# The last feed-forward layer computed in two halves of the tokens, the second half laid between the expert rows

## The reference

```
first_block, twice: x = x + gate * rmsnorm(mixer(h), ...)         # short convolution, then a state-space mixer
                    h = rmsnorm(x, norm_g[i, 2]) * (1 + scale) + shift
                    y = swiglu_ffn(h, f_w_in[i], f_w_out[i])      # width 2816: silu(gate) * up, then back to 1024
                    x = x + gate * rmsnorm(y, norm_g[i, 3])
second_block:       x = x + gate1 * (concat(band attention, gated delta rule) @ w_out)
                    h2 = modulate(rms_norm(x, norm2_gain), shift2, scale2)
                    x = x + gate2 * peer(h2, ...)
```

```
u = expert_down[experts];  vv = expert_up[experts]
act = gelu(einsum("thkd,td->thk", u, hb))
out = einsum("thk,thkd->td", gates * act, vv)
```

## Time and profile before

| | |
|---|---|
| median of 3 runs | 3354.09 us (3353.31 to 3354.44) |
| the profiled execution: span | 3351.2 us, 2.9 us less than the median of the timed runs |
| TensorE busy | 2945.8 us, 88% |
| VectorE busy | 2119.7 us, 63% |
| ScalarE busy | 1400.0 us, 42% |
| GpSimd busy | 652.5 us, 19% |
| read from memory | 793.46 MB, of it 536.90 MB by the gathers |

### The profile page before, as it was taken

How to read it: one execution, slowest core, us unless ns; L and a number is a source line. 1 busy time by engine, 2 the same in 40 slices (tenths; PEclk the granted TensorE clock), 3 DMA queues, 4 the chain that set the end, 5 groups by cost and what they waited for, 6 DMA issues and landing times.

```text
span 3351.2 us, 34609 instructions
## 1 busy us (share of the span) xinstructions
PE 2945.8 (88%) x11990; PEld 2050.0 (61%) x11990; DVE 2119.7 (63%) x3960; ACT 1400.0 (42%) x2879; POOL 652.5 (19%) x575
## 2 busy tenths in 40 slices
PE   6989999899998899998988998878879777777777
PEld 5868888688776688887777753656547232223222
DVE  7655443587786444432552999879669889655555
ACT  3243222444665422224733367772443433333333
POOL 0000000000111000000000133334443444443442
PEclk8999999999998999998998999989989899999999
DMA  6544444244122244442202597989999999999998
GB/s 251 184 144 135 142 141 145 85 151 132 58 70 95 95 139 148 144 129 98 98 26 87 220 371 267 355 341 387 412 420 417 353 421 422 421 422 421 421 421 335
DMA packets 147548, 797.82 MB, mean 238 GB/s; under 512 B 16304, under 2 KB 18480, under 8 KB 81712
## 3 DMA queue, kind: packets, MB, share of 16 engines
q0 software_dynamic: 73728, 536.90, 39.5%
q1 hardware_dynamic: 69840, 251.69, 22.6%
q10 hardware_dynamic: 3808, 7.02, 0.6%
HBM read 793.46 MB, written 2.10 MB: 237 GB/s over the span
## 4 chain that ended last, share of the span: by engine, by line
PE 52%; DMA 20%; DVE 18%; ACT 6%; issue 4%; POOL 0%; DVEq 0%; SPq 0%; POOLq 0%; ACTq 0%
PE psum L153 51%; DMA tail<-in_experts,tail 19%; DVE tail L187 5%; DVE tail L170 2%; ACT L164 2%; DVE tail L182 2%; ACT arena L164 2%; DVE tail L193 1%; DVE arena L182 1%; DVE tail L190 1%; DVE region L170 1%; DVE rounded L170 1%; ACT tail L164 1%; DVE tail L205 1%; DVE tail L196 1%
## 5 line engine op out<-in xcount | busy, mean ns | idle before, releaser
L153 PE MATMUL psum<-tail,arena 128*128 128x256 f32 (+2 forms) x3584 | 1274.5, 505 | 256.2 <-ACT arena L164 235.5
L153 PE MATMUL psum<-rounded,rounded 128*128 128x512 f32 x5496 | 1278.6, 393 | 39.6 <-DVE rounded L182 22.6
L153 PEld LDWEIGHTS psum<-rounded,rounded 128*128 128x128 f32 x5496 | 1034.0, 189 | 262.5 <-issue 29.0
L153 PEld LDWEIGHTS psum<-tail,arena 128*128 128x128 f32 x3584 | 677.7, 199 | 806.1 <-issue 748.4
L187 DVE CUSTOM_DVE_ANT_0 tail<-tail 128x1024 f32<-128x1024 f32 x512 | 621.0, 1223 | 311.7 <-DMA tail<-in_experts,tail 310.4
L216 POOL DMA_INDIRECT tail<-in_experts,tail x512 | 583.6, 1140 | 1015.9 <-PE psum L153 747.0
L164 ACT ACTIVATE tail<-tail 128x1 f32<-128x1 f32 (+1 forms) x1057 | 266.8, 252 | 769.2 <-DVE tail L187 740.7
L170 DVE TENSOR_TENSOR rounded<-arena,rounded 128x1024 fp32r<-128x1024 f32 (+2 forms) x285 | 316.5, 1111 | 333.7 <-ACT rounded L164 333.5
L164 ACT ACTIVATE rounded<-arena 128x1024 fp32r<-128x1024 f32 (+2 forms) x317 | 292.1, 939 | 406.5 <-DVE arena L170 232.5
L164 ACT ACTIVATE arena<-psum 128x256 f32<-128x256 f32 (+2 forms) x210 | 97.5, 480 | 393.6 <-PE psum L153 392.9
L170 POOL TENSOR_TENSOR arena<-arena 128x512 f32<-128x512 f32 x32 | 47.1, 1473 | 1087.7 <-ACT arena L164 1087.7
(11 more groups left out here) (87 smaller groups left out, 1560.4 us busy)
## 6 DMA issues: line engine op xcount, KB each, us to landing
arena<-in_ada SPq DMA_DIRECT2D x136, 512.0 KB, 3.7
arena<-in_fin SPq DMA_DIRECT2D x88, 512.0 KB, 4.2
arena<-in_win SPq DMA_DIRECT2D x56, 512.0 KB, 3.3
arena<-in_fout SPq DMA_DIRECT2D x32, 512.0 KB, 4.1
arena<-in_mxbc SPq DMA_DIRECT2D x32, 512.0 KB, 3.7
arena<-in_pq SPq DMA_DIRECT2D x32, 512.0 KB, 7.8
arena<-in_ain SPq DMA_DIRECT2D x24, 512.0 KB, 4.7
arena<-in_mz SPq DMA_DIRECT2D x16, 512.0 KB, 3.8
```

The source lines that it names most:

```text
L153: return self.e.matmul(o, a, b, start=start, stop=stop, skip_group_check=skip)
```

## The change

- The layer's pieces come twice in the list, once for each half of 256 tokens, in another order: for each pair of tiles two gate pieces, two up pieces, and two pieces of the way back of the pair before. `fout2` holds the way back by its input tile, so that one piece feeds all 8 output tiles, whose sums stay in PSUM banks 4 to 7 through the whole half.
- `pe_half`, `act_half`, `dve_half` do the norm, the 66 pieces and the norm behind, in steps. Half 0 stands where the layer stood. Half 1 is put ahead of main 1, between the rows.
- In half 1, from the fourth piece on, GpSimd writes the low weight parts: `pool_low`, one behind each gather from row 3 to row 65. Loads that reuse a buffer wait for it.
- `steps_of` runs a step behind every row, not every second one, and ranking steps of chunk 1 behind every second row. `EARLY` goes from 6 to 8.
- Main 1 gets the ordinary norm in place of one prepared ahead. Chunk 0's and 1's scores move to ring buffers 5 and 6, so the ring has 6 buffers until row 80 and 7 until row 190. `own_add` gives VectorE other rows. The table of levels is loaded again for main 1.

The diff, cut to its core:

```diff
+        HALF = []
+        for j in range(KF // 2):
+            HALF += [("gate", 2 * j), ("gate", 2 * j + 1), ("up", 2 * j), ("up", 2 * j + 1)]
+            if j:
+                HALF += [("out", 2 * j - 2), ("out", 2 * j - 1)]
+        HALF += [("out", KF - 2), ("out", KF - 1)]
+        SPLIT = list(range(len(PIECES)))
         for f in range(2):
+            if f:
+                AGAIN = len(SPLIT)
+            for what, kk in HALF:
+                SPLIT.append(len(PIECES))
+                piece(("half", f, what, kk), t["fout2"][kk] if what == "out" else t["fin"][1, 2 * kk + (what == "up")])
             for n in range(12):
...
@@ -369,16 +382,31 @@
         former = lambda i: i - 8 if i < 20 else i - 4

         w_in = landed("w_landed", 8)
-        w_hi, w_lo, gemm = signal("w_hi"), signal("w_lo"), signal("gemm")
+        w_hi, w_lo, w_lo_pool, gemm = signal("w_hi"), signal("w_lo"), signal("w_lo_pool"), signal("gemm")
         ada_step, ada_mm, mod_ok = signal("ada_step"), signal("ada_mm"), signal("mod_ok")
         col_in, const_in, x_in = landed("col_landed"), landed("const_landed"), landed("x_landed")
         csil_ok = signal("csil")
         nxt = {}

         def w_tile(p):
-            i = 2048 * (p % 3)
+            q = SPLIT_NO[p]
+            i = 2048 * (q % 3)
             n = 128 * PIECES[p][1]
-            return i, n
+            wf, wr = (w_f, w_r) if q < AGAIN else (w1_f, w1_r)
+            return wf[:, i:i + n], wr[:, i:i + n], wr[:, i + 1024:i + 1024 + n]
+
+        def by_pool(p):
+            return SPLIT_NO[p] >= AGAIN + 3
+
+        def low_at(p):
+            return w_lo_pool.at(p) if by_pool(p) else w_lo.at(p)
+
+        def pool_low(e, p):
+            n = 128 * PIECES[p][1]
+            high, _, low = w_tile(p)
+            e.wait_ge(*w_in.at(("w", p)))
+            e.wait_ge(*w_hi.at(p))
+            e.tt(low, raw[slot_of(NUMBER["w", p])][:, 0:n], high, ALU.subtract).then_inc(*w_lo_pool.tick(p))

         def sp_load(e, i):
             kind, n = LOADS[i]
...
-                    e.wait_ge(*(w_lo.at(m) if m < NSPLIT else gemm.at(m)))
+                    e.wait_ge(*(low_at(m) if m in SPLIT_NO else gemm.at(m)))
...
         def act_ahead(e):
-            p = nxt["act"]
-            if p >= NSPLIT:
+            q = nxt["act"]
+            if q >= len(SPLIT):
                 return
             nxt["act"] += 1
-            i, n = w_tile(p)
+            p = SPLIT[q]
+            n = 128 * PIECES[p][1]
             e.wait_ge(*w_in.at(("w", p)))
-            if p >= 3:
-                e.wait_ge(*gemm.at(p - 3))
-            e.act(w_r[:, i:i + n], raw[slot_of(NUMBER["w", p])][:, 0:n], ACT.Copy).then_inc(*w_hi.tick(p))
+            if q >= AGAIN + 3 or 3 <= q < AGAIN:
+                e.wait_ge(*gemm.at(SPLIT[q - 3]))
+            if q >= AGAIN:
+                e.wait_ge(*gemm.at(pc["pq", 0, 15]))
+                e.wait_ge(*tk_pe.at((1, 1)))
+            e.act(w_tile(p)[1], raw[slot_of(NUMBER["w", p])][:, 0:n], ACT.Copy).then_inc(*w_hi.tick(p))
...
-                if p >= NSPLIT:
-                    return
-                i, n = w_tile(p)
+                if p not in SPLIT_NO or by_pool(p):
+                    continue
+                n = 128 * PIECES[p][1]
+                high, _, low = w_tile(p)
                 e.wait_ge(*w_hi.at(p))
-                e.tt(w_r[:, i + 1024:i + 1024 + n], raw[slot_of(a)][:, 0:n], w_f[:, i:i + n],
-                     ALU.subtract).then_inc(*w_lo.tick(p))
+                e.tt(low, raw[slot_of(a)][:, 0:n], high, ALU.subtract).then_inc(*w_lo.tick(p))
                 return

...
-        SB = [over[:, 2048:4096], over[:, 0:2048]]
+        SB = [ring_mem[5], ring_mem[6], over[:, 2048:4096], over[:, 0:2048]]
...
+        def pe_half_out(e, f, kk):
+            p = pc["half", f, "out", kk]
+            j, u = kk // 2, kk % 2
+            _, hi, lo = [tiles(a, 8) for a in w_tile(p)]
+            e.wait_ge(*low_at(p))
+            e.wait_ge(*ga.done(("hg", f, j)))
+            a, b = a2r[:, j % 2, half_of(u)], b2r[:, j % 2, half_of(u)]
+            for d in range(8):
+                if kk == 0 and d % 2 == 0:
+                    ps.claim(("hy", f, d // 2), (4 + d // 2,))
+                    e.wait_ge(*ps.vacant(("hy", f, d // 2)))
+                o = ps["hy", f, d // 2][:, half_of(d % 2)]
+                e.mm(o, hi[:, d, :], a, kk == 0 and d % 2 == 0, False, True)
+                e.mm(o, hi[:, d, :], b, False, False, True)
+                last = kk == KF - 1 and d % 2 == 1
+                ins = e.mm(o, lo[:, d, :], a, False, last, True)
+                if last and d < 7:
+                    ins.then_inc(*hy_ok.tick((f, d // 2)))
+            ins.then_inc(*gemm.tick(p))
+
...
+        def pe_half(e, f):
+            yield from pe_norm(e, 3, f)
+            for s, (what, kk) in enumerate(HALF):
+                p = pc["half", f, what, kk]
+                if what == "out":
+                    pe_half_out(e, f, kk)
+                else:
+                    key = what, f, kk // 2
+                    if kk % 2 == 0:
+                        ps.claim(key, (2,) if what == "gate" else (3,))
+                        e.wait_ge(*ps.vacant(key))
+                    pe_gemm(e, p, ps[key][:, half_of(kk % 2)], lambda k: (h2r[:, k, :], l2r[:, k, :]),
+                            ready=h_ready(f) if s == 0 else None)
+                pe_after(e, p, (0, 1))
+                yield
+            o = ps.claim(("hs", f), (2,))
+            e.wait_ge(*ps.vacant(("hs", f)))
+            for b in range(4):
+                pe_pair_stat(e, ("hs", f, b), o[:, 0:256], ones, b == 0, b == 3)
+            yield
+            yield
...
+                        e.wait_ge(*gemm.at(pc["pq", 0, 15]))
+                        e.wait_ge(*tk_pe.at((1, 1)))
+                    e.wait_ge(*dve_b.at(("tn", 3, f, k)))
+                    e.act(h2r[:, k, :], hb(f, k), ACT.Identity, bias=shift(3, k)).then_inc(*h_hi.tick((3, f, k)))
+                yield
+            for s, (what, kk) in enumerate(HALF):
+                p = pc["half", f, what, kk]
+                if s + 3 < len(HALF):
+                    act_ahead(e)
+                j = gate_of_pair(what, kk)
+                if j is not None:
+                    key = "hg", f, j
+                    g = ga.claim(key, (0, 1, 2))
+                    e.wait_ge(*ga.vacant(key))
+                    e.wait_ge(*gemm.at(p))
...
+                ins = e.act(y2[:, k, :], ps["hy", f, k // 2][:, half_of(k % 2)], ACT.Copy, scale=post(3, k))
+                if k % 2:
+                    ins.then_inc(*ps.release(("hy", f, k // 2)))
+                if k == 3:
+                    act_rstd(e, ("hs", f), ("hs", f, 3), D, rst[1][:, 0:256], 256)
+            yield
+            yield
+
...
+                    dve_half_low(e, f, made)
+                if f == 0 and s + 3 < len(HALF):
+                    dve_ahead(e)
+                made = up_of_pair(what, kk)
+                if made is not None:
+                    g = ga["hg", f, made]
+                    e.wait_ge(*ps.done(("gate", f, made)))
+                    e.wait_ge(*gemm.at(pc["half", f, what, kk]))
+                    e.tt(g, ps["up", f, made], g, ALU.mult).then_inc(*ps.release(("up", f, made)))
+                dve_after(e, pc["half", f, what, kk])
+                yield
...
+        def dve_half_low(e, f, j):
+            e.wait_ge(*a_hi.at((f, j)))
+            e.tt(b2r[:, j % 2, :], ga["hg", f, j], a2f[:, j % 2, :], ALU.subtract).then_inc(*ga.release(("hg", f, j)))
...
-            yield from wait_steps(2) if f else pe_norm(e, 4, f)
+            yield from pe_norm(e, 4, f)
...
             yield from pe_wo(e, f)
             yield from pe_norm(e, 5, f)
...
-        FROM, FROM_LAST = 150, 260
-        turn_of, slot_no, last_use, prev = list(range(NRING)), [], {}, []
+        FROM_SEVENTH, FROM, FROM_LAST = 80, 190, 260
+        turn_of, slot_no, last_use, prev = list(range(NRING - 1)), [], {}, []
         for n in range(512):
+            if n == FROM_SEVENTH:
+                turn_of = [NRING - 1] + turn_of
...
             s = n % 128
-            if n < 192:
-                return s % 2 == 1 and (16 <= s if n >= 128 else 48 <= s < 124)
-            return 16 <= s < 124 and s % (8 if n < 256 else 16) == 1
+            return 16 <= s < 124 and s % (4 if n < 72 else 2 if n < 192 else 8 if n < 256 else 16) == 1
...
+                if n == FROM_SEVENTH:
+                    e.wait_ge(*idx_ok.at((1, 3)))
...
+                if 3 <= n < len(HALF):
+                    pool_low(e, SPLIT[AGAIN + n])
...
-        EARLY, LEFT = 6, 9
+        EARLY, LEFT = 8, 9
...
         def steps_of(c, grp, main, ranks):

             if c < 2 and next(main, True) is None:
-                some(ranks, 1 + grp % 2 if c == 0 else 0)
-            else:
+                some(ranks, grp % 2 if c == 0 else 0)
+            elif grp % 2:
                 some(ranks, 2 if c == 1 else 1)

...
```

(7 more changed lines are left out.)

206 lines of the change are left out of this document (114 added, 92 removed).

## The result

The changed kernel took 3393.57 us, median of 4 runs (3390.13 to 3395.36); the kernel before, beside it, 3354.27 (4 runs, 3353.31 to 3354.48). The ratio is 1.0117, 95% interval 1.0103 to 1.0131: 39 us slower. The forecast was 3412, its range 3345 to 3475.

What follows compares the result with a forecast made beforehand. TensorE was taken to bound the kernel ahead of 1914 us, no single engine among the first rows, gathers from 2690 us. 1752 to the first dot + 890 + 758 + 9 = 3409 span, forecast 3412 us, range 3345 to 3475.

Steps and rivals of the forecast that it cites:

- first dot: Start of the first row's dot, forecast at 1752 us: 1914 less 169 gained in front, plus 7 on VectorE.
- rows 0 to 65: Rows each carrying one piece of the layer's second half, forecast at 4.9 us a row, 323 us.
- rows 66 to 199: Rows each carrying a step of norm, then main 1; forecast in parts of 50, 70, 220, 148 and 80 us.
- Ahead of the rows: The layer's first half in front of the rows: 200 us instead of 369, at 0.12 us a matmul.
- third rival: Half-width matmuls cost their weight load: 0.069 us more each, 109 us added twice, 3630 us; chance 0.02.
- TensorE's work: TensorE's sum over rows 0 to 200: 765 us, taken as 890 at a share of 0.86.
- sign of being wrong: Forecast is wrong if TensorE stands above 0.93 through rows 0 to 200, or first dot comes later than 1780 us.
- first rival: TensorE packs the rows: at a share of 0.95 the 765 us take 805, giving 3327 us; chance 0.18.
- the loop: Beside the second half: gather, dot, gate, rounding, low part, later gather; 15.8 us in four rows, 4.0 a row.
- Tail: After row 200: ring about 10 rows ahead, 302 gathers remaining at 2.51 us, 758 us.
- DMA: Second weight reading, 34.6 MB or 82 us at 421 GB/s, hidden in rows 0 to 65 unless under 3.7 us each.
- Second rival: GpSimd and VectorE stop each other: 6 us a row, rows 0 to 65 take 396 us, total 3485; chance 0.22.

Runs made afterwards that it cites:

- e10: Changed kernel, an eighth of each second-half weight tile loaded and one of three products left out in its 44 gate and up pieces; 3378.91 us, ratio 1.0072.
- e6: Changed kernel, one of three products left out in the second half's 44 gate and up pieces, loads unchanged; 3385.78 us, ratio 1.0099.
- e3: Changed kernel, every fourth row from row 68 on takes no step of the last token layer; 3362.67 us, ratio 1.0031.
- e9: e3 with every third row, not every fourth, taking no step from row 128 on; 3350.60 us, ratio 0.9989.
- e12: e3 with every second row stepless from row 102 to 155, every fourth from 156 to 203, every third from 204; 3342.70 us, ratio 0.9964.
- e11: e9 with 24, not 8, second-half steps ahead of the first row, last token layer spread over more rows; 3355.49 us, ratio 1.0004.
- e2: Changed kernel, whole second half run before the first row, low parts on VectorE, steps in two of three rows; 3471.69 us, ratio 1.0350.

## Why the prediction was right

The direction and the main reason held. The size came out 18 us too large (a span of 3409 was forecast and 3390.6 measured), and that is the sum of errors of both signs: first dot 0.5 us sooner, rows 0 to 65 38.5 less, rows 66 to 199 2 more, what lies behind row 200 17 more (and 1 from rounding its parts, 891, to 890). That it came so near is in part luck. Rows 0 to 199 of after, by the starts of the dots (1751.5, 2036.0 and 2606.4 us for rows 0, 66 and 200):

```profile
1751.50:2606.40 854.90, 767.66 (x3874) 569.08 (x3873) 657.85 (x1326) 490.89 (x997) 379.33 (x266) 0.95 0.85 320
```

- *Ahead of the rows: right.* The half took 0.12 us a matmul, its first row with GpSimd idle and TensorE at 199.72 of 200. The third rival is out. Main 0's first product came 166.7 us earlier (169 said), the first dot at 1751.5 (1752 said).
- *TensorE's work right, its share too low.* Its sum was 765 us and 767.7 was measured, but in 855 us and not 890: a share of 0.90. The prediction had both values, 0.86 from the first rows and 0.90 from main 0, and chose the first. Its sign of being wrong, above 0.93 through rows 0 to 200, did not come.
- *Rows 0 to 65: too dear by 38 us.* This is the term of the sum that was mis-sized. Said 4.9 us a row, which is TensorE's 4.5 at a share of 0.92; measured 284.5 us, 4.3 a row, with TensorE busy 4.24 of it, 0.98. The first rival's mechanism, TensorE packing the rows, was true here for more than half of the chain. The bound by the loop, 4.0 us a row, was near too, and e10 with TensorE relieved comes down to 4.2. Two of the loop's terms missed in opposite ways: the gathers landed in 8.6 us (median in e6; 7.0 said), and the low part took 2.0:

```profile
L170 POOL TENSOR_TENSOR rounded<-arena,rounded x63: 1995/2012/2706, 1754.9 to 2025.1; 128x1024 fp32r<-128x1024 f32 x63
```

  The 2.68 us came from carrying on the rise of 0.69 us per 256 columns in the earlier trace rows; from 512 to 1024 columns it rose by 0.71 us in all. A gather on GpSimd, put at 0.94, took 1.38 on the mean in 1751 to 2025 us. GpSimd's 3.5 us a row come near the 3.9 said, by two errors that partly cancel.
- *Rows 66 to 199: right in sum, not in parts.* Said 568 us, measured 570. Part by part (norm, then to row 100, 140, 180 and 200) it was 50, 70, 220, 148 and 80 said and 47, 81, 205, 140 and 97 measured. That three engines of equal load hand each other work, with none above 0.91 of any stretch in the table, is what 2025 to 2600 us shows.
- *Tail: too good by 17 us.* 2.51 us a row held. But when row 200's dot began, 7 later gathers had been issued and not 10 (in 2450 to 2600 us the buffers came free late), and from there to the end it took 784 us, not 767.
- *DMA: nearly hidden, with less room than said.* The second reading of the weights filled the DMA engines to 0.93, not 0.75. In part the rows came quicker; in part weight loads fill the engines more than the sum had it, which priced them at the gathers' 421 GB/s. In the earlier trace rows the layer's loads move 131 GB/s at a share of 0.41, which makes 320 at a full one. An estimate from that: 34.6 MB are 108 us of all DMA engines, not 82, and the rows could not fall under 4.1 us, not 3.7. Loading an eighth of it gave 6 us.
- *One reading was off.* In the earlier trace rows the DMA engines do not stand at eight to ten tenths in all of the last 18 slices (slice 22 has five, slice 24 seven); nothing in the sum hangs on it.
- *Second rival: right on the mechanism, wrong on its price.* The two engines do exclude each other, which cost about 43 us of VectorE's time, but that didn't make the rows 6 us long. Taking GpSimd out lost 72 us.
- The rule that I quoted from the Trainium skill (GPSIMD Engine Reference, Key points: GpSimd and VectorE contend for SBUF when a VectorE instruction has two SBUF inputs) agrees with these rows: two inputs in SBUF stretch, one in PSUM doesn't. The Trainium skill's page SBUF — State Buffer (SBUF: two separate sides) adds that the pair of ports is held for a whole instruction and that the later one waits; the 3.02 us dot and the 25 others that began inside a low part agree.
- *What the prediction did not see* is that the loss lay in the pace: the 58 us were worked out for one step in every row, and fewer steps a row weren't priced. e3, e9 and e12 took back 31, 43 and 51 us. The move itself about breaks even in the balance under e11.

What remains open: what the loop of rows 0 to 65 costs by itself, what the move is worth at an equal pace, and the 17 us in e2.

## What to carry to other kernels

Before you move work beside a stream that is fed by memory, ask whether the engines have room there. If several engines of like load stand between, the move can return only what it saves (here the first dot came 165 us sooner and the rows took 165 us longer). What could then be won was in the number of items that share the crowded stretch, since each item left to the memory-bound tail costs its full transfer time, and in giving the dearest steps the most of them.

A unit that is busy 0.99 of a stretch may be one limit of several. Two tests go together: take work from it and see whether the items come quicker, and follow the chain that ended last, before and after, to see what took its place.

## What was unexpected of the hardware

- A GpSimd subtraction of 1024 columns into fp32r took 2.0 us (median), 1.55 times the 1.30 us of 512 columns in the earlier trace rows. The five with no VectorE instruction beside them took as long, 2.00 us.
- Beside GpSimd's sums VectorE's two-input operations wait out the whole sum (a dot of 1.22 us took 3.02); with an input in PSUM they kept their 0.69 us. Two inputs aren't needed for it: three one-input `TENSOR_SCALAR` of 32 uint32 that began inside a low part took 1.37, 1.97 and 1.97 us and ended 0.04 us behind it, where four others took 0.18 to 0.25. The waits of dots and ranking sums cost 43 of 274 us, and the order of the queues mattered more than that: with the low parts on VectorE 14 rows fewer passed.
- The matmul of 256 columns took half of the time of the 512-wide one (1652 records in 200 us, 0.12 us each, against 0.230) though each has a weight load of its own. The granted clock was 0.99, at the 2.4 GHz level; the loads were busy 199.37 of the 200 us beside the products and did not lengthen them.
